# Causal attention in a two-block kernel: scores laid out with keys on the partitions instead of queries

## The chip, the cores and the metric

The program runs on 1 core of one Trainium2 chip. The metric is the device time of one execution in microseconds (us); lower is better.

## The reference, cut to what matters

The kernel computes two blocks in float32: first a mixer of two linear recurrences over 2048 tokens, then a block with latent attention, a spatial gating unit and an output projection. Only the attention of the second block is touched. It has 8 heads; a query or key of a head has 64 + 32 = 96 entries, a value 64:

```python
def one_block(args):
    qi, i = args
    sc = jnp.einsum('bqhd,bkhd->bhqk', qi, k).astype(jnp.float32) * scale
    qpos = i * Q_BLOCK + jnp.arange(Q_BLOCK)
    mask = kpos[None, :] <= qpos[:, None]
    sc = jnp.where(mask[None, None], sc, -jnp.inf)
    p = jax.nn.softmax(sc, axis=-1).astype(v.dtype)
    return jnp.einsum('bhqk,bkhd->bqhd', p, v)
```

## The kernel before, in words

The program is a row of phases, each a block of its own in which the engines run hand-written queues, with semaphores between them. `phase_attention` is the last but one; `phase_output` follows when it has ended. A helper `Stages` gives each step of an engine a number on that engine's semaphore; a `wait_ge(X.sem, X.at(0, name))` waits for the step called `name`. Eight PSUM banks of 512 float32 columns are shared out by hand.

`phase_attention` first makes all values (`vall`, line 3161), then works through four pairs of heads. For a pair it projects queries and keys ("P": 8 ring items of 128x512, lines 3170 and 3174, copied to `qT` and `kT` by ScalarE at line 3244). Its scores ("S", line 3187) have 128 queries on the partitions and up to 512 keys as columns; p counts pairs of query blocks, e the two heads of the pair, r the two query blocks. VectorE takes each piece out of PSUM, scales it and keeps a maximum per query (L3308), adds the causal mask to the diagonal piece (L3313), and reduces the maxima (L3317, L3320). ScalarE takes the exponent of a whole row of pieces at once, with the maximum as its bias and the row's sum as a by-product (L3253). The rest of the work ("R") turns each 128x128 tile of exponents on TensorE (L3204), so that keys come to the partitions, copies it to SBUF on ScalarE (`pT`, L3266), and multiplies it with the values (L3217). The two heads' results go to the two halves of a bank's partitions. At the end of an R the reciprocals of the sums are spread by four small matmuls (L3222), copied (L3274) and multiplied onto the result (L3327).

The order of S and R steps is written out by hand and alternates long and short rows, so that VectorE and ScalarE work on the scores of one step while TensorE turns and multiplies those of another. Three banks hold scores (`NS`), three hold turned tiles (`NTB`), two hold results. GpSimd has nothing to do in this phase but to build the mask.

## Time and profile before

| what | value |
|---|---|
| median of 3 runs | 4113.3 us (4111.99 to 4114.04) |
| the profiled execution, its own time | 4112.49 us |
| its span, first to last instruction | 4110.8 us |
| TensorE busy in the span | 3831.5 us, 93% |
| VectorE, ScalarE, GpSimd busy | 2097.6 us, 1295.6 us, 705.6 us |
| TensorE's mean granted clock | 0.970 |

Times below are microseconds from the span's start. Engines: PE is TensorE's matmul queue, PEld its weight loads, DVE VectorE, ACT ScalarE, POOL GpSimd, SP the queue that issues DMAs. A float32 matmul shows as two records; a transpose as one. Records of matmuls overlap, so a busy time divided by the count, or the distance between starts, is a price, and the mean duration is not.

### The profile page before, as it was taken

To read this page: it belongs to the slowest core of one execution; us is meant where nothing else is said; L and a number is where in the kernel's file an instruction comes from. 1 tells how busy PE (TensorE), PEld (TensorE's weight loads), DVE (VectorE), ACT (ScalarE), POOL (GpSimd) and SP (SyncE) were. 2 spreads that over 40 slices of the span, in tenths; PEclk is the share of its full clock that TensorE was granted. 3 is DMA by queue.
4 is the path that set the end of the run, shared out by engine and by line. 5 is a ranking of instruction groups with operands and counts; after the bars stand their busy time and mean duration, and the time that the engine had idled before them with its cause. 6 is when DMAs were issued, how large, how long until landed. Compare 5 with 4: busy or idle time off the path is not lost. (4 is left out here: it accounts for less than half of the span.)

```text
span 4110.8 us, 48844 instructions
## 1 busy us (share of the span) xinstructions
PE 3831.5 (93%) x18971; PEld 1967.7 (48%) x18971; DVE 2097.6 (51%) x3541; ACT 1295.6 (32%) x2539; POOL 705.6 (17%) x660
## 2 busy tenths in 40 slices
PE   6999899998799989999999899898989799999898
PEld 3444354454577764444444344344544355555443
DVE  7688337543566656122227767524445343443377
ACT  3333132553455547111110001111221355555400
POOL 0000010000566640032114231212200000000031
PEclk8999999999999999999999999899989999999999
DMA  5222582576555544122325633321120000000133
GB/s 192 47 51 48 99 175 81 131 130 114 167 170 172 173 130 139 62 87 82 125 83 175 200 118 108 118 82 41 41 62 12 22 1 8 8 1 6 69 121 108
DMA packets 590152, 386.33 MB, mean 94 GB/s; under 512 B 412019, under 2 KB 525783, under 8 KB 586979
## 3 DMA queue, kind: packets, MB, share of 16 engines
q1 hardware_dynamic: 573059, 315.57, 27.9%
q0 software_dynamic: 10336, 42.47, 2.9%
q10 hardware_dynamic: 6528, 25.17, 1.5%
q8 instruction: 152, 2.49, 0.3%
q14 instruction: 77, 0.63, 0.1%
HBM read 252.59 MB, written 130.55 MB: 93 GB/s over the span
## 5 line engine op out<-in xcount | busy, mean ns | idle before, releaser
L635 PE MATMUL bank<-uT,front_W 128*128 128x512 f32 (+1 forms) x1216 | 488.0, 563 | 4.9 <-ACT front_b_ L842 4.9
L567 PE MATMUL bank<-uT,front_W 128*128 128x512 f32 (+1 forms) x896 | 363.1, 563 | 0.0
L635 PEld LDWEIGHTS bank<-uT,front_W 128*128 128x128 f32 x1216 | 231.9, 192 | 252.5 <-issue 246.1
L567 PEld LDWEIGHTS bank<-uT,front_W 128*128 128x128 f32 x896 | 169.8, 191 | 182.8 <-issue 179.5
L3187 PE MATMUL bank<-kT,attn_qT 96*128 96x512 f32 (+3 forms) x640 | 250.1, 543 | 7.4 <-ACT kT L3244 6.8
L1613 PE MATMUL bank<-uT 128*128 128x512 f32 x512 | 224.3, 596 | 4.3 <-PEq L1186 4.3
L3266 ACT ACTIVATE attn_pT<-bank 128x512 f32<-128x512 f32 (+1 forms) x288 | 157.6, 574 | 124.9 <-PE bank L3204 123.4
L3187 PEld LDWEIGHTS bank<-kT,attn_qT 96*128 96x128 f32 x640 | 114.8, 192 | 131.7 <-issue 76.7
L1312 POOL TENSOR_TENSOR scan_U<-scan_U,gla_w 128x512 f32<-128x512 f32 x144 | 146.7, 1039 | 167.8 <-DVE scan_U L1500 167.8
L3217 PE MATMUL bank<-attn_pT,uT 128*64 128x256 f32 (+1 forms) x1152 | 169.2, 389 | 6.4 <-ACT attn_pT L3266 6.4
L3308 DVE TENSOR_SCALAR_CACHE_REDUCE attn_sc_big<-bank 128x512 f32<-128x512 f32 (+1 forms) x208 | 126.0, 627 | 89.5 <-PE bank L3187 87.5
L3327 DVE TENSOR_TENSOR uT<-bank,attn_spread 128x256 f32<-128x256 f32 x32 | 13.6, 425 | 288.3 <-ACT attn_spread L3274 288.3
L1613 PEld LDWEIGHTS bank<-uT 128*128 128x128 f32 x512 | 96.5, 191 | 119.9 <-issue 119.9
L1302 POOL TENSOR_TENSOR scan_SP<-scan_S,eGl 128x512 f32<-128x512 f32 x144 | 146.6, 1039 | 26.2 <-DVE scan_S L1519 19.7
L1012 DVE RECIPROCAL front_q<-front_q 128x2048 f32<-128x2048 f32 (+1 forms) x8 | 110.0, 13752 | 47.5 <-ACT front_q L789 47.5
L3253 ACT ACTIVATE attn_sc_big<-attn_sc_big,attn_top 128x1920 f32<-128x1920 f32 (+3 forms) x64 | 104.3, 1629 | 94.8 <-DVE attn_top L3320 94.8
L3415 POOL TENSOR_TENSOR out_S<-uT,out_b 128x512 f32<-128x512 f32 x8 | 10.1, 1264 | 709.2 <-DVE uT L3495 709.2
L3204 PE MATMUL bank<-ident,attn_sc_big 128*128 128x128 f32 x800 | 126.2, 286 | 1.2 <-ACT attn_sc_big L3253 1.2
L1519 DVE TENSOR_TENSOR scan_S<-scan_SP,bank 128x512 f32<-128x512 f32 x144 | 92.5, 684 | 63.2 <-PE bank L1394 63.2
L1004 DVE SCALAR_TENSOR_TENSOR front_work<-front_work,front_taps 128x2308 f32<-128x2308 f32 (+1 forms) x48 | 121.6, 2533 | 1.7
L1785 PE MATMUL bank<-yT,merge_S 128*128 128x512 f32 x256 | 117.7, 603 | 4.0 <-POOL merge_S L1772 4.0
L3204 PEld LDWEIGHTS bank<-ident,attn_sc_big 128*128 128x128 f32 x800 | 86.3, 142 | 68.5 <-issue 55.0
(546 smaller groups left out, 6937.3 us busy)
## 6 DMA issues: line engine op xcount, KB each, us to landing
scan_gq<-gla_asks_keys_values SPq DMA_DIRECT2D x36, 768.0 KB, 7.6
scan_dq<-delta_qkv SPq DMA_DIRECT2D x32, 768.0 KB, 6.3
merge_gates<-merge_r ACTq DMA_DIRECT2D x16, 1024.0 KB
uT<-merge_gates SPq DMA_DIRECT2D x16, 1024.0 KB, 9.0
gla_asks_keys_values<-front_a SPq DMA_DIRECT2D x14, 1152.0 KB, 11.2
front_W<-in_w_in SPq DMA_DIRECT2D x28, 512.0 KB, 10.7
delta_qkv<-front_b_ SPq DMA_DIRECT2D x8, 1152.0 KB, 9.9
gla_asks_keys_values<-front_b_ SPq DMA_DIRECT2D x8, 1152.0 KB, 17.7
```

The lines of the kernel that those rows point to most:

```text
L567: m = pe.matmul(bank[:, conv_bank(f, b), 0:n], W[:, f % 2, k, :], uT[:, k, t0:t0 + n], start=(k == 0), stop=(k == KT - 1))
L635: mm = pe.matmul(bank[:, b, 0:n], W[:, s, k, :], uT[:, k, t0:t0 + n], start=(k == 0), stop=(k == KT - 1))
L1004: dve.scalar_tensor_tensor(out=acc[:, lo:WIDE], in0=raw[:, f % 2, lo + t:t + WIDE], scalar=tap[:, t:t + 1], in1=acc[:, lo:WIDE], op0=ALU.m ...
L1302: nc.gpsimd.tensor_tensor(SP[d][:], S[d][:], bcast(gl, 2, P), ALU.mult).then_inc(GS(f"SP{d}"), 1)
L1312: nc.gpsimd.tensor_tensor(U[d][:], U[d][:], bcast(w, 2, P), ALU.mult).then_inc(GU(f"U{d}"), 1)
L1613: mm = pe.matmul(bank[:, b, :], W[f % 2][:, k, :], uT[:, k, CTX + b * BANK:CTX + (b + 1) * BANK], start=(k == 0), stop=(k == KT - 1))
L1785: mm = pe.matmul(bank[:, spot(q, name), :], left[:, k, :], right(k), start=(k == 0), stop=(k == H - 1))
L3187: pe.matmul(bank[:, SC0 + ring[name] % NS, 0:hi - lo], qT[:, e, i * P:(i + 1) * P], kT[0:QK, e, lo:hi], start=True, stop=True).then_inc(TS ...
L3204: m = pe.transpose(bank[:, TB0 + n % NTB, (2 * e + r) * P:(2 * e + r + 1) * P], tile_of(p, e, r)[:, c * P:(c + 1) * P], chip.ident[:])
L3217: m = pe.matmul(bank[e * DV:(e + 1) * DV, ob, r0:2 * P], vall[:, c, h * DV:(h + 1) * DV], pT[:, n % NTB, e, r0:2 * P], start=(c == 0), sto ...
L3266: act.activation(pT[:, n % NTB, :, r0:2 * P], bank[:, TB0 + n % NTB, :].rearrange("p (e t) -> p e t", e=2)[:, :, r0:2 * P], ACT.Copy).then ...
L3308: m = dve.tensor_scalar(t[:, g * BANK:g * BANK + w], bk[:, 0:w], SCALE, None, ALU.mult, ALU.max, accum_out=mx[:, s, u, plain:plain + 1])
```

## The change

The scores of `phase_attention` are made the other way round: 128 keys (a chunk c) on the partitions, and up to 512 queries (a quarter B of the sequence) as columns. The work is cut into 32 units (`UNITS`), each one head and one quarter, in the order B = 3, 0, 3, 0, 2, 1, 2, 1 in each pair of heads; a unit has 4(B + 1) chunks, the last four of them cut to 512, 384, 256 and 128 columns by the causal edge. For each chunk:

- TensorE makes the scores in one of four ring banks (`NS = 4`);
- VectorE adds the mask in PSUM to the first 128 columns of an edge chunk, then takes an elementwise maximum of the chunk with a running one in `mx`;
- ScalarE copies the scores to SBUF; only this frees the ring bank.

At the end of a unit's scores TensorE turns the four 128-wide parts of `mx` (`turn`), VectorE reduces them to one exact maximum per query (`top`), and TensorE spreads these to a full bank (`tops`). Then, again per chunk, VectorE subtracts that bank from the scores, ScalarE takes the exponent with the scale, GpSimd adds the exponents into `acc` (512 wide, one add after the other), and TensorE multiplies them with the values, queries as columns, in two halves of 256. After the last chunk `total` sums `acc` over the partitions with a matmul against ones, and VectorE's `out` takes a 256-wide reciprocal and multiplies it onto both halves.

The values of unit u are interleaved with the scores of unit u + 1 (`merged` for TensorE; `led` for VectorE and ScalarE, four chunks ahead). `total` of unit u stands in the middle of unit u + 1, `out` of unit u at its end. The tile that holds the scores and exponents is one of two, `sc[u % 2]`; the ScalarE copy of unit u's first chunk therefore waits for the last value matmul and the last GpSimd add of unit u - 2.

```diff
-    NS, NTB = 3, 3
-    SC0, TB0, OB0 = 0, 3, 6
-    BIG, SMALL = QT // 2 - 1, QT // 4 - 1
+    PER_B = BANK // P
+    HB = BANK // 2
+    NS, TB, MB, OB = 4, 4, 5, 6
+    AHEAD = 4
+    UNITS = [(h, B) for a in range(PAIRS) for h, B in ((2 * a, 3), (2 * a, 0), (2 * a + 1, 3), (2 * a + 1, 0),
+                                                      (2 * a, 2), (2 * a, 1), (2 * a + 1, 2), (2 * a + 1, 1))]
+    NU = len(UNITS)
+    chunks = lambda B: range(PER_B * (B + 1))
+
+    def cut(B, c):
+
+        d = max(0, c - PER_B * B)
+        start = min(c, PER_B * B) * BANK + sum(BANK - n * P for n in range(d))
+        return d * P, start, BANK - d * P
+    size = lambda B: sum(cut(B, c)[2] for c in chunks(B))
+
+    def items(u):
+
+        if u == NU:
+            return []
+        h, B = UNITS[u]
+        first = [("proj", k, h // 2, b) for b in range(NB) for k in "qk"] if u % (NU // PAIRS) == 0 else []
+        return first + [("score", u, c) for c in chunks(B)]
+
+    def merged(u):
+
+        X, Y = items(u + 1)[3:], [("value", u, c) for c in chunks(UNITS[u][1])]
+        R, X = X[:3], X[3:]
+        while X or Y:
+            if X and (not Y or len(X) * len(chunks(UNITS[u][1])) >= len(Y) * max(1, len(items(u + 1)) - 6)):
+                R.append(X.pop(0))
+            else:
+                R.append(Y.pop(0))
+        R.insert(len(R) // 2, ("sum", u - 1))
+        return R
+
+    def led(u):
+
+        Y = [("value", u, c) for c in chunks(UNITS[u][1])]
+        lead = Y[:AHEAD]
+        R = merged(u)
+        out, early = [], 0
+        for x in R:
+            if x[0] == "value":
+                if x[2] + AHEAD < len(Y):
+                    out.append(Y[x[2] + AHEAD])
+            elif x[0] != "sum":
+                if early < len(lead):
+                    out.append(lead[early])
+                    early += 1
+                out.append(x)
+            if x[0] == "value" and early < len(lead):
+                at = len(out) - (1 if x[2] + AHEAD < len(Y) else 0)
+                out[at:at] = lead[early:]
+                early = len(lead)
+        return out
+
+    ring_items = [x for u in range(-1, NU) for x in items(u + 1)]
+    ring = {x: i for i, x in enumerate(ring_items)}
+    name = lambda x: "_".join(str(v) for v in x)
...
-        sc = [sb("sc_big", [P, 2, (4 * BIG + 3) * P]), sb("sc_small", [P, 2, (4 * SMALL + 3) * P])]
-        pT = sb("pT", [P, NTB, 2, 2 * P])
-        mx = sb("mx", [P, 2, 4, 5])
-        top, total, share = (sb(n, [P, 2, 4]) for n in ("top", "total", "share"))
-        spread = sb("spread", [P, 2 * P])
+        sc = [sb("sc_big", [P, size(3)]), sb("sc_small", [P, size(1)])]
+        mx = sb("mx", [P, 2, BANK])
+        acc = sb("acc", [P, 2, BANK])
+        top = sb("top", [P, 2, PER_B])
+        share = sb("share", [P, HB])
...
-        order = []
-        for a in range(PAIRS):
-            order += [("P", a, 0), ("S", a, 7)] + ([("R", a - 1, 3)] if a else [])
-            order += [(x, a, p) for x, p in (("S", 0), ("R", 7), ("S", 6), ("R", 0), ("S", 1), ("R", 6), ("S", 5), ("R", 1),
-                                            ("S", 2), ("R", 5), ("S", 4), ("R", 2), ("S", 3), ("R", 4))]
-        order.append(("R", PAIRS - 1, 3))
...
+        def piece(x):
+            _, u, c = x
+            lo, start, w = cut(UNITS[u][1], c)
+            return lo, sc[u % 2][:, start:start + w], w
+        spot = lambda x: ring[x] % NS
 
...
-                                    pattern=[[-1, P]], channel_multiplier=1).then_inc(mask_ready, 1)
+                                    pattern=[[1, P]], channel_multiplier=-1).then_inc(mask_ready, 1)
+            for u in range(NU):
+                for c in chunks(UNITS[u][1]):
+                    x = ("value", u, c)
+                    lo, p, w = piece(x)
+                    if c == 0 and u >= 2:
+                        pool.wait_ge(TH.sem, TH.at(0, str(u - 2)))
+                    if c:
+                        pool.wait_ge(GP.sem, GP.at(0, name(("value", u, c - 1))))
+                    pool.wait_ge(AX.sem, AX.at(0, name(x)))
+                    if c:
+                        pool.tensor_tensor(acc[:, u % 2, lo:BANK], acc[:, u % 2, lo:BANK], p, ALU.add).then_inc(GP(name(x)), 1)
+                    else:
+                        pool.tensor_copy(acc[:, u % 2, :], p).then_inc(GP(name(x)), 1)
 
...
-            def rest(a, p):
...
-                                m = pe.transpose(bank[:, TB0 + n % NTB, (2 * e + r) * P:(2 * e + r + 1) * P],
-                                                 tile_of(p, e, r)[:, c * P:(c + 1) * P], chip.ident[:])
...
+            def item(x):
+                n = ring[x] - NS
+                if n >= 0:
+                    pe.wait_ge(AE.sem, AE.at(0, name(ring_items[n])))
...
+                    m = pe.matmul(dst[:, 0:w], kT[0:QK, h % 2, c * P:(c + 1) * P], qT[:, h % 2, B * BANK + lo:(B + 1) * BANK],
                                   start=True, stop=True)
...
+            def turn(u):
+                pe.wait_ge(DM.sem, DM.at(0, name(("score", *last_of(u)[1:]))))
+                if u:
+                    pe.wait_ge(DT.sem, DT.at(0, str(u - 1)))
+                else:
+                    pe.wait_ge(vall_copied, QT)
+                for t in range(PER_B):
+                    m = pe.transpose(bank[:, TB, t * P:(t + 1) * P], mx[:, u % 2, t * P:(t + 1) * P], chip.ident[:])
+                m.then_inc(TT(str(u)), 1)
+
+            def tops(u):
+                pe.wait_ge(DT.sem, DT.at(0, str(u)))
+                if u:
+                    pe.wait_ge(DS.sem, DS.at(0, name(last_of(u - 1))))
+                for t in range(PER_B):
+                    m = pe.matmul(bank[:, MB, t * P:(t + 1) * P], top[:, u % 2, t:t + 1].broadcast_to([P, P]), chip.ident[:],
+                                  start=True, stop=True)
+                m.then_inc(TM(str(u)), 1)
+
+            def value(x):
+                _, u, c = x
+                h, B = UNITS[u]
+                lo, p, w = piece(x)
+                pe.wait_ge(AX.sem, AX.at(0, name(x)))
+                if c == 0 and u >= 2:
+                    pe.wait_ge(DO.sem, DO.at(0, str(u - 2)))
+                for half in range(2):
+                    q0 = max(lo, half * HB)
+                    if q0 < (half + 1) * HB:
+                        m = pe.matmul(bank[half * DV:(half + 1) * DV, OB + u % 2, q0 - half * HB:HB],
+                                      vall[:, c, h * DV:(h + 1) * DV], p[:, q0 - lo:(half + 1) * HB - lo], start=(c == 0),
+                                      stop=(c == PER_B * B + 2 * half + 1))
+                m.then_inc(TO(name(x)), 1)
+
+            def total(u):
+                if u < 0:
+                    return
+                pe.wait_ge(GP.sem, GP.at(0, name(last_of(u))))
+                for half in range(2):
+                    m = pe.matmul(bank[half * DV:(half + 1) * DV, OB + u % 2, HB:BANK], chip.ones[:, 0:DV],
+                                  acc[:, u % 2, half * HB:(half + 1) * HB], start=True, stop=True)
+                m.then_inc(TH(str(u)), 1)
+
+            for x in items(0):
+                item(x)
+            for u in range(NU):
+                X = items(u + 1)
+                for x in X[:1]:
+                    item(x)
+                turn(u)
+                for x in X[1:3]:
+                    item(x)
+                tops(u)
+                for x in merged(u):
+                    if x[0] == "value":
+                        value(x)
+                    elif x[0] == "sum":
+                        total(x[1])
+                    else:
+                        item(x)
+            total(NU - 1)
 
...
-            def exponents(a, p, tiles):
...
-                    act.activation(t, t, ACT.Exp, bias=top[:, slot(p), u], accum_out=total[:, slot(p), u]
...
-            def rest(a, p, scored):
...
+                    _, u, c = x
+                    lo, p, w = piece(x)
+                    if c == 0 and u >= 2:
+                        act.wait_ge(TO.sem, TO.at(0, name(last_of(u - 2))))
+                        act.wait_ge(GP.sem, GP.at(0, name(last_of(u - 2))))
+                    act.wait_ge(DM.sem, DM.at(0, name(x)))
+                    m = act.activation(p, bank[:, spot(x), 0:w], ACT.Copy)
+                m.then_inc(AE(name(x)), 1)
+
+            for x in items(0):
+                item(x)
+            for u in range(NU):
+                for x in items(u + 1)[:3]:
+                    item(x)
+                for x in led(u):
+                    if x[0] == "value":
+                        lo, p, w = piece(x)
+                        act.wait_ge(DS.sem, DS.at(0, name(x)))
+                        act.activation(p, p, ACT.Exp, scale=SCALE).then_inc(AX(name(x)), 1)
+                    else:
+                        item(x)
 
...
-            def rest(a, p):
...
+            def item(x):
+                if x[0] == "proj":
+                    return
+                _, u, c = x
+                h, B = UNITS[u]
+                lo, p, w = piece(x)
+                d = c - PER_B * B
+                bk = bank[:, spot(x), 0:w]
+                dve.wait_ge(TS.sem, TS.at(0, name(x)))
+                if d >= 0:
+                    dve.tensor_tensor(bk[:, 0:P], bk[:, 0:P], ahead[:], ALU.add).then_inc(DK(f"{u}_{d}"), 1)
+                    dve.wait_ge(DK.sem, DK.at(0, f"{u}_{d}"))
+                if c:
+                    dve.wait_ge(DM.sem, DM.at(0, name(("score", u, c - 1))))
+                    dve.tensor_tensor(mx[:, u % 2, lo:BANK], bk, mx[:, u % 2, lo:BANK], ALU.max).then_inc(DM(name(x)), 1)
+                else:
+                    dve.tensor_copy(mx[:, u % 2, :], bk).then_inc(DM(name(x)), 1)
+
+            def out(u):
+                if u < 0:
+                    return
+                h, B = UNITS[u]
+                dve.wait_ge(TH.sem, TH.at(0, str(u)))
+                if u:
+                    dve.wait_ge(DO.sem, DO.at(0, str(u - 1)))
+                dve.reciprocal(share[:], bank[:, OB + u % 2, HB:BANK]).then_inc(DH(str(u)), 1)
+                dve.wait_ge(DH.sem, DH.at(0, str(u)))
+                e = h % 2
+                for half in range(2):
+                    rows = slice(half * DV, (half + 1) * DV)
+                    m = dve.tensor_tensor(oT[e * DV:(e + 1) * DV, h // 2, B * BANK + half * HB:B * BANK + (half + 1) * HB],
+                                          bank[rows, OB + u % 2, 0:HB], share[rows, :], ALU.mult)
+                m.then_inc(DO(str(u)), 1)
+
+            for x in items(0):
+                item(x)
+            for u in range(NU):
+                X = items(u + 1)
+                for x in X[:1]:
+                    item(x)
+                dve.wait_ge(TT.sem, TT.at(0, str(u)))
+                dve.tensor_reduce(top[:, u % 2, :], bank[:, TB, :].rearrange("p (t k) -> p t k", k=P), mybir.AxisListType.X, ALU.max
+                                  ).then_inc(DT(str(u)), 1)
+                for x in X[1:3]:
+                    item(x)
+                dve.wait_ge(TM.sem, TM.at(0, str(u)))
+                for x in led(u):
+                    if x[0] == "value":
+                        lo, p, w = piece(x)
+                        dve.wait_ge(AE.sem, AE.at(0, name(("score", *x[1:]))))
+                        dve.tensor_tensor(p, p, bank[:, MB, lo:BANK], ALU.subtract).then_inc(DS(name(x)), 1)
+                    else:
+                        item(x)
+                out(u - 1)
+            out(NU - 1)
```

## Rows read from the trace of the kernel before

**Rows 1.** Window over the phase: PE, PEld, DVE, ACT, POOL busy, granted clock.
```profile
3259.80:3884.80 625.00, 609.13 (x3233) 328.30 (x3231) 258.59 (x1024) 359.50 (x642) 0.00 (x0) 0.99 0.02 4
```

**Rows 2.** TensorE's groups in the phase: count, busy us, mean ns.
```profile
L3204 PE MATMUL bank<-ident,attn_sc_big 128*128 128x128 f32 x800 | 126.2, 286 | 1.2 <-ACT attn_sc_big L3253 1.2
...
L3222 PE MATMUL bank<-ident,attn_share 128*64 128x128 f32 x256 | 21.0, 279 | 0.0
...
L3187 PE MATMUL bank<-kT,attn_qT 96*128 96x128 f32 x64 | 12.8, 282 | 0.2 <-DVE attn_sc_big L3313 0.2
```

**Rows 3.** Timeline of TensorE: start, us, engine, line, instructions merged.
```profile
3259.82 1.88 PE L3170 MATMUL bank<-cqT,attn_WQ 128*128 128x512 f32 x4
3261.53 1.02 PE L3174 MATMUL bank<-ckvT,attn_WK 128*128 128x512 f32 x2
...
3420.70 15.24 PE L3187 MATMUL bank<-kT,attn_qT 96*128 96x512 f32 x32 [1.70 <-ACT kT L3244]
...
3878.28 0.66 PE L3204 MATMUL bank<-ident,attn_sc_small 128*128 128x128 f32 x4
3878.87 0.65 PE L3217 MATMUL bank<-attn_pT,uT 128*64 128x256 f32 x4
3879.45 0.66 PE L3204 MATMUL bank<-ident,attn_sc_small 128*128 128x128 f32 x4
```

**Rows 4.** VectorE's groups, by form, whole span.
```profile
L3313 DVE SCALAR_TENSOR_TENSOR attn_sc_big<-bank,attn_ahead 128x128 f32<-128x128 f32 x64 | 18.3, 287 | 0.0
...
L3327 DVE TENSOR_TENSOR uT<-bank,attn_spread 128x256 f32<-128x256 f32 x32 | 13.6, 425 | 288.3 <-ACT attn_spread L3274 288.3
...
L3031 DVE RECIPROCAL latents_v<-latents_v 128x1024 f32<-128x1024 f32 x4 | 26.2, 6553 | 0.1
...
L3325 DVE RECIPROCAL attn_share<-attn_total 128x4 f32<-128x4 f32 x32 | 5.4, 168 | 0.0
```

**Rows 5.** Timeline in the scans, GpSimd and VectorE side by side.
```profile
1319.24 2.04 POOL L1312 TENSOR_TENSOR scan_U<-scan_U,gla_w 128x512 f32<-128x512 f32 x2 [2.46 <-DVE scan_U L1500]
...
1320.54 1.28 DVE L1519 TENSOR_TENSOR scan_S<-scan_SP,bank 128x512 f32<-128x512 f32 x2 [0.85 <-PE bank L1394]
```

**Rows 6.** ScalarE's groups of the phase, by form.
```profile
L3266 ACT ACTIVATE attn_pT<-bank 128x512 f32<-128x512 f32 x256 | 146.5, 598 | 118.2 <-PE bank L3204 116.7
...
L3253 ACT ACTIVATE attn_sc_small<-attn_sc_small,attn_top 128x512 f32<-128x512 f32 x8 | 5.8, 720 | 0.0
...
L3253 ACT ACTIVATE attn_sc_small<-attn_sc_small,attn_top 128x128 f32<-128x128 f32 x8 | 3.2, 396 | 0.0
```

**Rows 7.** GpSimd: timeline of the output phase; L3417 needs L3415's result.
```profile
3912.48 1.27 POOL L3415 TENSOR_TENSOR out_S<-uT,out_b 128x512 f32<-128x512 f32 x1 [3.37 <-DVE uT L3495]
3913.83 1.27 POOL L3417 TENSOR_TENSOR out_S<-out_S,uT 128x512 f32<-128x512 f32 x1
```

**Rows 8.** GpSimd at half the width, by form.
```profile
L482 POOL TENSOR_TENSOR front_work<-front_neg_beta,ctri 128x256 f32<-128x256 f32 x18 | 12.5, 718 | 593.1 <-DVE front_neg_beta L1068 511.1 <-DMA delta_blocks<-front_work 82.0
```

**Rows 9.** Windows of 2 us; granted clock third from last.
```profile
3422.00:3424.00 2.00, 2.00 (x4) 0.85 (x3) 1.32 (x4) 0.00 (x0) 0.00 (x0) 0.60 0.00 0
3424.00:3426.00 2.00, 2.00 (x4) 0.97 (x3) 0.88 (x3) 0.00 (x0) 0.00 (x0) 0.55 0.00 0
...
3578.00:3580.00 2.00, 2.00 (x6) 0.95 (x5) 1.74 (x5) 0.00 (x0) 0.00 (x0) 1.00 0.02 4
```

**Rows 10.** Windows of 4 us after the phase's end.
```profile
3888.00:3892.00 4.00, 0.00 (x0) 0.00 (x0) 1.23 (x1) 0.00 (x0) 0.54 (x1) 0.50 1.05 362
...
3896.00:3900.00 4.00, 4.00 (x6) 1.68 (x5) 0.20 (x1) 0.00 (x0) 0.50 (x1) 0.50 1.04 387
```

**Rows 11.** Timeline, output phase: VectorE adds from SBUF alone, without and with GpSimd.
```profile
3902.46 2.29 DVE L3560 TENSOR_TENSOR out_WT<-uT,out_WT 128x2048 f32<-128x2048 f32 x1 [0.38 <-DMA uT<-in_w_out]
...
3902.57 6.55 POOL L3426 TENSOR_TENSOR uT<-uT 128x2048 f32<-128x2048 f32 x1 [6.07 <-DMA uT<-in_w_out]
...
3904.86 6.40 DVE L3563 TENSOR_TENSOR out_WT<-uT,out_WT 128x2048 f32<-128x2048 f32 x1
```

230 lines of the change are left out of this document (44 added, 186 removed).

## Prediction, made before the changed kernel ran

> **What bounds the kernel now.** I read the page's engine shares first (TensorE 93% busy), then the windows over the attention phase, then its groups, then timelines for the spacing of starts. Attention lasts from 3259.8 to 3884.8 us: 625 us, of which TensorE is busy for 609, ScalarE for 360, VectorE for 259 and GpSimd for none [rows 1]. TensorE sets the pace; in 625 us it is without work for 16. The other phases are not touched, so the change is worth what it does to these 625 us.
>
> **TensorE's work.** The scores have as many columns as before (136 x 128 per head, 320 matmuls), and the values too (two streams to two halves of the partitions, as now). A 512-column matmul costs 0.86 us, since the four records of a projection start 1.71 us before the next [rows 3]. A step of four value records costs 0.58 and a step of four turns 0.59 by their starts [rows 3]. What goes: 1088 turns, of which the 800 in the first row cost 126 us busy [rows 2]; by the starts 0.146 each, 159 us. Also the 32 spreads of shares (21 us busy, 19 after overlap) [rows 2]. What comes, for each of 32 units: four turns of the maxima (0.6); four 128x128 spreads of them, eight records between 0.08 (share spreads, 64 columns wide) and 0.2 us (128-column scores) [rows 2], that is 0.7 to 1.6, taken at 1.2 because the full width loads twice the weights of the one; and a sum of the exponents (0.6). That is 2.4 a unit, 77 in all. TensorE: 609 - 159 - 19 + 77 = 508 us.
>
> **VectorE's work.** Each chunk costs a maximum and a subtraction, each with one PSUM input. The trace has this shape: two 512-wide adds with a PSUM input in 1.28 us [rows 5], 0.64 each; 128 columns take 0.29 [rows 4]; between them I interpolate 0.40 and 0.52. Then 224 x 0.64 + 96 x 0.40 = 181 us, twice: 363. The 128 mask additions, each followed by a wait for itself, 0.33: 42. Per unit a reduction over 512 columns (0.69), two 256-wide multiplications (0.43 each) and a 256-wide reciprocal. Today's reciprocals are 4 wide (0.17 us); one of 1024 takes 6.55 [rows 4], so 256 columns cost about 0.17 + 252 x 6.26 ns = 1.75. That is 3.3 a unit, 105 in all. VectorE: 510 us, nearly TensorE's 508, where it now has 259.
>
> **ScalarE and GpSimd.** A copy of 512 columns takes 0.60, an exponent 0.72 and a 128-wide one 0.40 [rows 6]: copies 172, exponents 209, projections 38, together 419 us. GpSimd: an add that needs the one before starts 1.35 us after it [rows 7]; 256 columns take 0.72 [rows 8]. The scans' adds take 1.02 each, with one operand broadcast [rows 5]. The changed adds have two full operands and form a chain through `acc`, so I take 1.35 and keep 1.02 as the lower bound. 192 full adds, 96 narrow ones at 0.8 and 32 copies at an estimated 0.6 are 357 us. No engine is over-full, but the queues are in order, so the units have to be walked.
>
> **One boundary.** Let 0 be VectorE's last maximum of a unit's scores. VectorE is next in `out` of an older unit (1.75 + 0.85 = 2.6), then takes the next unit's first maximum (0.65), so `top` is ready at 4.0. TensorE, which by then has done the turn and two scores, idles 1.5 to 2 us. VectorE's next two maxima and TensorE's `tops` both end at about 5.4, the subtraction at 6.1, the first exponent at 6.8. Where the next unit starts with an edge chunk its masks add 0.5: 7.3.
>
> **Units B = 3 with scores B = 0 (8 of them).** From 5.9 VectorE subtracts a chunk every 0.65 and ScalarE exponentiates one every 0.72: all 16 are out by about 18.5. GpSimd needs 0.6 + 12 x 1.35 + 2.5 = 19.3 from 7.3 on and ends at 26.6. Behind it stands ScalarE: its first copy of the unit after next reuses the tile, so it waits until 26.6. Its queue then holds all exponents, too. TensorE can put four scores in the ring and stops at about 21; VectorE stops as well. From 27 on TensorE has the rest of the B = 3 scores (9.0), the four values (1.7) and a sum (0.65): 11.4, and with VectorE's last maximum the pair of units takes 39.2. Where scores B = 2 follow it is four scores less: 35.8.
>
> **The other units.** v2 with scores 1, and v1 with scores 2: VectorE's sums are 15.9 each, boundary included, with the last hand-overs 16.3, 17.2 and 16.4 (GpSimd's lag, 5 us after the first of them, costs 1 in the second). v1 with projections and scores 3: TensorE 30.7, walked 31. One pair of heads: 39.2 + 35.8 + 16.3 + 17.2 + 16.4 + 31 = 155.9. All: projections and first scores 26, four pairs 623.6, less the last 31, plus a tail of 18, less 3 (no `out` in the first unit): 634 us at full clock. Taken with adds at 1.02, the eight B = 3 units give back 8 x 12 x 0.33 = 32: 602.
>
> **TensorE's clock.** Now it is granted 0.99 over the phase [rows 1], for it hardly idles. After the 1.70 us gap at 3419 the clock showed 0.60 and 0.55 for two windows of 2 us [rows 3, 9]; after an equal gap at 3576 it stayed at 1.00 [rows 9]. At half clock (1.2 instead of 2.4 GHz) such a stretch of some 3 us costs 1.4 us of work. After the long pause behind the phase the clock was at 0.50, and still there in the first 4 us of continuous work [rows 10]. The change makes one gap of 1.5 to 2 us in each of 32 units and one of about 5.5 behind each of the 8 long chains of adds. The long ones end where TensorE has the critical part, at 2.4 each (4 us and somewhat more at half clock): 8 x 2.4 = 19. Of the short ones I take half, and of these only some 4 us in all, since in most units VectorE or GpSimd is the longer: 22 together, bounds 0 and 45. The Trainium skill ("TensorE: Matmul & The Clock Gate", section on HAM oscillation) speaks against the change: it says that waits between short blocks of matmuls re-throttle the engine, so that every block begins cold. The trace bears that out for one of the two equal gaps named here. With that rule at all 32 boundaries the sum would be near the upper bound instead of 22.
>
> **The sum.** 634 + 22 = 656 against 625: +31. The profiled execution took 4112.5, 0.8 under the median of 4113.3; with 1.7 outside its span that does not change. 4112.5 + 31 = 4143.5, rounded to 4144.
>
> **Edits at no cost.** The mask's other triangle is built once, before the phase's first score, behind the value matmuls; were it not covered it would be under 1 us. SP's DMAs are the same; their waits name the same moments (last projection, last score of a pair). The wait for the rotated queries existed before (part of the 1.70 us gap).
>
> **Rivals.**
> - *The accumulation hides, and the time falls* (0.24). One mechanism: GpSimd's chain of adds keeps up with the exponents. For it: GpSimd's total is 357 of more than 550 us, and the scans show 1.02 for an add [rows 5]. Against: dependent adds with two full operands are at 1.35 [rows 7]. It decides where an add costs under about 0.85, or where the tile's next use came later than walked. Then units 1 to 4 take VectorE's 16.3 each: 155.9 - (75 - 65.2) = 146 a pair, 595; with queues that slide ideally VectorE's 510 plus four projections at 10: 550. At little clock loss 595 gives 4082, 550 gives 4038; the middle, 4060.
> - *Everything cancels* (0.08): adds at 1.02 and the clock's 22 give 624: 4111.
> - *The clock falls at every boundary* (0.10): 32 x 1.4 instead of the short gaps' 4, and the long ones 19 to 25: about +65 to +75, 4185.
> - *VectorE and GpSimd get in each other's way* (0.03). A VectorE add with both inputs in SBUF took 2.29 us alone and 6.40 beside a GpSimd add that took 6.55 [rows 11]. If it were so here, VectorE's 363 us and GpSimd's 357 would queue behind one another: some 170 more than VectorE's bound, 4240 or above. Against: with one PSUM input both kept their price side by side [rows 5], and the change has no VectorE operation with two SBUF inputs. The Trainium skill ("GPSIMD Engine Reference", SBUF interfaces) says the same: contention comes with two SBUF inputs or a 2-port mode. By that rule the sum stays as it is.
>
> **Chances and range.** My forecast has 0.55, for 4122 to 4175: below by adds at 1.2 us, above by 45 us of clock losses. Faster 0.24, same 0.08, clock 0.10, contention 0.03. A change within 0.2% (8 us) can't be told from none. Slower: 0.55 + 0.10 + 0.03 = 0.68. Eight in ten: from 4068 (leaves out half of the faster cases) to 4190 (most of the clock case is in).
>
> **What would show it.** Right: ScalarE's copy from PSUM waits on GpSimd in 8 units, those that follow a B = 3, for 4 to 8 us; GpSimd at 1.3 us per add; the reciprocal at 1.75 us; VectorE busy for about 510 us of the phase and TensorE for about 510 plus what the clock adds, granted clock 0.93 to 0.97. Wrong: waits on GpSimd under 2 us (the first rival), VectorE's 512-wide operations above 0.8 us beside GpSimd (the last), or a reciprocal that is a lot cheaper, which would shorten each boundary and VectorE's total by up to 50 us.

## The result, and the profile after

The changed kernel takes 4209.4 us (median of 4 runs, 4203.16 to 4221.19) against 4113.3 (4111.99 to 4114.04): ratio 1.0237, 95% interval 1.0214 to 1.026. It is 96 us slower, 65 more than forecast and beyond the range's upper end of 4190. The profiled execution, read below, is the fastest of the four (4203.16).

The window over the attention phase, with its last reductions (the columns are those of [rows 1]):

```profile
3261.00:3975.00 714.00, 595.35 (x2401) 279.71 (x2399) 491.81 (x896) 366.10 (x706) 333.21 (x320) 0.87 0.02 4
```

The phase lasts 713.9 us, from 3261.0 to 3974.9; it was 625 [rows 1]. TensorE is busy for 595 of them, but at a granted clock of 0.87: part of that is work at half clock (1.2 instead of 2.4 GHz). VectorE went from 259 to 492. No engine is full any more.

The groups of the phase, by form, answering to [rows 2, 4, 6, 7]:

```profile
L3218 PE MATMUL bank<-attn_qT,kT 96*128 96x512 f32 x448 | 261.0, 705 | 57.5 <-ACT attn_sc_big L3307 47.1 <-ACT kT L3298 10.3
L3183 POOL TENSOR_TENSOR attn_acc<-attn_acc,attn_sc_big 128x512 f32<-128x512 f32 x160 | 203.7, 1273 | 22.5 <-ACT attn_sc_big L3319 11.4
L3341 DVE TENSOR_TENSOR attn_mx<-bank,attn_mx 128x512 f32<-128x512 f32 x192 | 132.7, 691 | 124.9 <-PE bank L3218 121.2
L3377 DVE TENSOR_TENSOR attn_sc_big<-attn_sc_big,bank 128x512 f32<-128x512 f32 x176 | 109.7, 679 | 2.8 <-PE bank L3237 2.8
L3319 ACT ACTIVATE attn_sc_big<-attn_sc_big 128x512 f32<-128x512 f32 x176 | 106.4, 630 | 9.4 <-DVE attn_sc_big L3377 8.6
L3307 ACT ACTIVATE attn_sc_big<-bank 128x512 f32<-128x512 f32 x176 | 103.0, 600 | 227.4 <-POOL attn_acc L3183 113.6 <-DVE attn_mx L3341 103.5 <-DVE attn_mx L3343 7.1
L3352 DVE RECIPROCAL attn_share<-bank 128x256 f32<-128x256 f32 x32 | 56.0, 1749 | 3.9 <-PE bank L3261 3.9
```

The last part of a row is the idle time in front of the group. In all, ScalarE's copies (L3307) stood 114 us behind GpSimd's adds (L3183) and 104 behind maxima. The scores (L3218) stood 47 us behind those copies; the same 448 records cost 261 us here and 222 in a variant at clock 0.96 (experiment 4).

The timeline of one unit, the first B = 3, after its scores had ended at 3286 (columns as in [rows 3]):

```profile
3293.04 7.46 ACT L3319 ACTIVATE attn_sc_big<-attn_sc_big 128x512 f32<-128x512 f32 x15
...
3293.81 18.54 POOL L3183 TENSOR_TENSOR attn_acc<-attn_acc,attn_sc_big 128x512 f32<-128x512 f32 x15 [0.17 <-ACT attn_sc_big L3319]
...
3312.44 1.57 ACT L3307 ACTIVATE attn_sc_big<-bank 128x512 f32<-128x512 f32 x3 [11.94 <-POOL attn_acc L3183]
3313.09 5.05 PE L3218 MATMUL bank<-attn_qT,kT 96*128 96x512 f32 x6 [6.28 <-ACT attn_sc_big L3307]
```

This is the walk's central picture. ScalarE has all exponents out at 3300.5, GpSimd adds them until 3312.4, ScalarE's next copy waits 11.9 us for the tile, and TensorE 6.3 us for the copy. Eight chains end like this one, and TensorE's stalls behind them last 4.9 to 6.3 us, 44 in all. TensorE then needs 5.05 us for six records that take 2.84 at full clock: it came back at half speed. Windows around that restart (granted clock third from last), and around the same restart in the third pair of heads:

```profile
3313.00:3315.00 2.00, 1.91 (x3) 0.88 (x4) 0.00 (x0) 2.00 (x6) 0.41 (x1) 0.50 0.00 0
3315.00:3317.00 2.00, 2.00 (x4) 0.97 (x3) 1.11 (x3) 1.32 (x4) 1.23 (x3) 0.50 0.00 0
3317.00:3319.00 2.00, 2.00 (x7) 0.49 (x6) 1.49 (x3) 0.90 (x3) 1.12 (x2) 0.86 0.00 0
...
3659.00:3661.00 2.00, 1.95 (x3) 0.92 (x4) 0.00 (x0) 2.00 (x6) 0.38 (x1) 0.50 0.00 0
3661.00:3663.00 2.00, 2.00 (x4) 0.93 (x3) 1.15 (x3) 1.29 (x3) 1.23 (x2) 0.50 0.00 0
3663.00:3665.00 2.00, 2.00 (x6) 0.30 (x4) 1.18 (x3) 0.79 (x2) 1.18 (x2) 0.50 0.01 4
3665.00:3667.00 2.00, 2.00 (x6) 0.84 (x3) 0.27 (x1) 0.60 (x1) 0.00 (x0) 0.50 0.00 0
3667.00:3669.00 2.00, 2.00 (x3) 0.34 (x1) 0.69 (x1) 0.60 (x1) 0.00 (x0) 0.50 0.00 0
3669.00:3671.00 2.00, 2.00 (x9) 0.94 (x8) 0.69 (x1) 0.60 (x1) 0.00 (x0) 0.50 0.01 4
3671.00:3673.00 2.00, 2.00 (x4) 1.03 (x4) 0.02 (x1) 0.00 (x0) 0.00 (x0) 0.61 0.00 0
3673.00:3675.00 2.00, 2.00 (x6) 0.57 (x4) 1.67 (x3) 1.03 (x2) 0.00 (x0) 1.00 0.00 0
```

The first restart is at full clock again after some 4.5 us. The second, after a gap of nearly the same length (6.08 us), keeps TensorE at 1.2 GHz for 13 us of continuous work. By the starts of `top`'s reductions (L3368) the units from there to the next ones last, in us:

| kernel | u0 | u1 | u2 | u3 | u4 | u5 | u6 | u7 | pair |
|---|---|---|---|---|---|---|---|---|---|
| forecast, full clock | u0+u1 39.2 | | u2+u3 35.8 | | 16.3 | 17.2 | 16.4 | 31 | 155.9 |
| after, pair 1 | 15.1 | 29.1 | 15.3 | 24.4 | 15.4 | 18.5 | 15.7 | 36.2 | 169.6 |
| after, pair 2 | 15.7 | 28.6 | 15.7 | 24.3 | 15.4 | 18.5 | 15.7 | 42.3 | 176.2 |
| after, pair 3 | 15.4 | 33.1 | 16.3 | 27.5 | 15.4 | 18.5 | 15.7 | 42.3 | 184.3 |

The granted clock is 0.7 to 0.9 in u0 to u3, 1.00 in u4 to u6, and in u7 1.00 in the first pair and 0.84 in later ones. Equal queues, unequal times: that is the clock's part. The rest is the same in every pair. The fourth pair repeats the third up to u5 and has no u7.

### The profile page after: what moved, and what is told of

Read it like the earlier page. It is cut to its first block and busy times, and to the rows that moved or that the text cites. A ratio compares the mean times of both kernels' runs of the same rounds, so it can differ in the third digit from the quotient of the medians.

```text
span 4201.5 us, 47760 instructions
## 1 busy us (share of the span) xinstructions
PE 3818.2 (91%) x18139; PEld 1918.9 (46%) x18139; DVE 2330.1 (55%) x3413; ACT 1301.2 (31%) x2603; POOL 1041.2 (25%) x980
## 5 line engine op out<-in xcount | busy, mean ns | idle before, releaser
L3218 PE MATMUL bank<-attn_qT,kT 96*128 96x512 f32 (+3 forms) x640 | 314.5, 615 | 57.5 <-ACT attn_sc_big L3307 47.1
L3183 POOL TENSOR_TENSOR attn_acc<-attn_acc,attn_sc_big 128x512 f32<-128x512 f32 (+3 forms) x208 | 238.4, 1146 | 26.2 <-ACT attn_sc_big L3319 11.4
L3341 DVE TENSOR_TENSOR attn_mx<-bank,attn_mx 128x512 f32<-128x512 f32 (+3 forms) x288 | 173.4, 602 | 128.2 <-PE bank L3218 121.2
L3218 PEld LDWEIGHTS bank<-attn_qT,kT 96*128 96x128 f32 x640 | 119.3, 211 | 181.6 <-issue 82.4
L3307 ACT ACTIVATE attn_sc_big<-bank 128x512 f32<-128x512 f32 x224 | 121.4, 554 | 243.0 <-DVE attn_mx L3341 117.9
L482 POOL TENSOR_TENSOR front_work<-front_neg_beta,ctri 128x256 f32<-128x256 f32 x18 | 12.5, 716 | 593.9 <-DVE front_neg_beta L1068 512.0
L1302 POOL TENSOR_TENSOR scan_SP<-scan_S,eGl 128x512 f32<-128x512 f32 x144 | 146.7, 1039 | 26.2 <-DVE scan_S L1519 19.7
L3251 PE MATMUL bank<-attn_sc_big,uT 128*64 128x256 f32 (+1 forms) x832 | 129.0, 433 | 22.9 <-ACT attn_sc_big L3319 22.8
L3377 DVE TENSOR_TENSOR attn_sc_big<-attn_sc_big,bank 128x512 f32<-128x512 f32 x224 | 126.2, 622 | 2.8 <-PE bank L3237 2.8
L3319 ACT ACTIVATE attn_sc_big<-attn_sc_big 128x512 f32<-128x512 f32 x224 | 121.9, 581 | 9.8 <-DVE attn_sc_big L3377 8.6
L1818 ACT ACTIVATE merge_r<-merge_r 128x1024 f32<-128x1024 f32 x32 | 33.7, 1052 | 268.4 <-DVE merge_r L1865 266.0
```

What stands on the lines that cost most here:

```text
L1302: nc.gpsimd.tensor_tensor(SP[d][:], S[d][:], bcast(gl, 2, P), ALU.mult).then_inc(GS(f"SP{d}"), 1)
L3183: pool.tensor_tensor(acc[:, u % 2, lo:BANK], acc[:, u % 2, lo:BANK], p, ALU.add).then_inc(GP(name(x)), 1)
L3218: m = pe.matmul(dst[:, 0:w], kT[0:QK, h % 2, c * P:(c + 1) * P], qT[:, h % 2, B * BANK + lo:(B + 1) * BANK], start=True, stop=True)
L3251: m = pe.matmul(bank[half * DV:(half + 1) * DV, OB + u % 2, q0 - half * HB:HB], vall[:, c, h * DV:(h + 1) * DV], p[:, q0 - lo:(half + 1) * ...
L3319: act.activation(p, p, ACT.Exp, scale=SCALE).then_inc(AX(name(x)), 1)
L3341: dve.tensor_tensor(mx[:, u % 2, lo:BANK], bk, mx[:, u % 2, lo:BANK], ALU.max).then_inc(DM(name(x)), 1)
```

## The experiments

Ratios are to the kernel before, with 95% intervals; times are medians. Kernels that build on one another show only the new edit.

**1. Idle time filled.** TensorE multiplies into banks that nobody reads at that moment, before `tops`, before the first values, in the stall and before the first score after projections, so that it never rests long:

```diff
+            def fill(n, bk):
+                for _ in range(n):
+                    pe.matmul(bank[:, bk, :], chip.ident[:], cqT[:, 0, 0:BANK], start=True, stop=True)
...
+                if u:
+                    pe.wait_ge(DS.sem, DS.at(0, name(last_of(u - 1))))
+                    fill(2, MB)
                 tops(u)
-                for x in merged(u):
+                for i, x in enumerate(merged(u)):
+                    if i == 1 and u + 1 < NU:
+                        if len(X) == PER_B:
+                            fill(2, TB)
+                        elif UNITS[u - 1][1] == 3:
+                            fill(7, TB)
+                    if x[0] == "score" and x[2] == 0:
+                        fill(3, TB)
```

> The changed kernel with idle-time matmuls added (all results kept): 2 before each spread of the maxima, 2 before the first value of a unit whose successor has quarter 0, 7 where the wait for GpSimd's chain is, 3 before the first score after projections; identity times 512 columns, into banks that are free there. Theory 'half clock is the missing term': the phase took 714 us where 634 were walked at full clock; the granted clock of the phase goes from 0.87 to above 0.97 and the time falls by 45 to 75 us, to 4135 to 4165. Rival 'the missing time is full-clock waiting, and the low clock only goes with it': the clock rises but the time falls by less than 20 us, or rises.

Measured: 4168.9, ratio 1.0139 (1.0124 to 1.0154). Its phase lasts 683 us, from 3258 to 3942; a window that begins 3 us late and ends 8 us behind it:

```profile
3261.00:3950.00 689.00, 649.54 (x2684) 300.35 (x2683) 491.46 (x897) 368.14 (x704) 334.61 (x321) 0.99 0.03 7
```

The clock is back at 0.99 and every pair lasts 169.8 us. Useless work makes the kernel 40 us faster, a little less than the 45 to 75 expected. Yet a pair is still 13.9 over the forecast, so the clock is not all, or the fills cost something themselves. Experiments 3 and 4 part the two.

**2. GpSimd's adds made cheap.** One column instead of up to 512, on a tile preset to ones; the sum of the exponents is left out.

```diff
-                        pool.tensor_tensor(acc[:, u % 2, lo:BANK], acc[:, u % 2, lo:BANK], p, ALU.add).then_inc(GP(name(x)), 1)
+                        pool.tensor_tensor(acc[:, u % 2, lo:lo + 1], acc[:, u % 2, lo:lo + 1], p[:, 0:1], ALU.add).then_inc(GP(name(x)), 1)
...
-                        pool.tensor_copy(acc[:, u % 2, :], p).then_inc(GP(name(x)), 1)
+                        nc.gpsimd.memset(acc[:, u % 2, :], 1.0).then_inc(GP(name(x)), 1)
```

> The changed kernel with GpSimd's adds 1 column wide instead of 512 to 128, on a tile preset to 1.0: this leaves out the sum of the exponents. All waits stay. Theory 'GpSimd's chain holds ScalarE': the 12 waits of ScalarE for GpSimd (113.6 us) go, the units behind quarter 3 fall from 28.6 to 33.1 and 24.3 to 27.5 us to some 17 to 20, and the time falls by 70 to 110 us, to 4100 to 4140. Rival 'VectorE and the hand-overs bound those units anyway': the time falls by less than 35 us.

Measured: 4112.7, ratio 1.0004 (0.9994 to 1.0013). The chain of adds, with what it does to the clock, is worth 97 us, as much as the whole slowdown. u1 and u3 fall to 20.3 and 16.0; u0 and u2 stay at 15.4 and 15.6. Not all is well without the chain: u7, with projections, lasts 41.1 to 42.5 at a clock of 0.84 to 0.88, where the first pair of the changed kernel had 36.2 at 1.00.

**3. Both.** Cheap adds, and the fills but for the seven in the stall, which no longer exists.

> The narrow adds and the added matmuls together, without the group of 7 (leaves out the sum of the exponents). If the clock is also lost without GpSimd's chain, in the short gaps at the boundaries, this is 15 to 40 us faster than narrow adds alone; if only the long waits bring the clock down, it is within 8 us of it or slower.

Measured: 4118.0, ratio 1.0016 (1.0007 to 1.0025), 5 us slower than without fills, at clock 1.00 in every unit. This is a balance, and no sign that the gaps cost nothing. By the starts of `top`'s reductions, the full clock makes u0 and u2 14.6 us long instead of 15.1 to 15.6 (7 us in eight units) and u7 37.9 instead of 41.1 to 42.5 (11 us in three). Against that u1, u3 and u5 each last 1.7 us longer (20 us in twelve), the time of the two fills in front of `tops`, and u6 0.5. So the short gaps behind which the clock falls cost some 0.8 us each, and the gap before the first score after projections costs more.

**4. Fills in the long gaps alone.** Six in the stall, two before the first score after projections, nothing at the boundaries.

```diff
+                        if len(X) > PER_B and UNITS[u - 1][1] == 3:
+                            fill(6, TB)
+                    if x[0] == "score" and x[2] == 0:
+                        fill(2, TB)
```

> The changed kernel with idle-time matmuls only in its long gaps (6 at the wait for GpSimd's chain, 2 before the first score after projections), none at the short gaps before the spread of the maxima and before the first value. All results kept. If the long gaps bring the clock down, this is at or below the 4169 of all fillings, with a granted clock of the phase above 0.95; if the short gaps do it as well, the clock of the phase stays near 0.9 and the time between 4175 and 4205.

Measured: 4151.7, ratio 1.0098 (1.0083 to 1.0113), 58 us faster than the changed kernel. Its phase, of 665.0 us (from 3258.3 to 3923.3), and two of its groups, the fills themselves being the second:

```profile
3258.20:3924.00 665.80, 592.19 (x2513) 284.27 (x2511) 490.27 (x896) 363.87 (x707) 333.90 (x320) 0.96 0.02 4
```
```profile
L3218 PE MATMUL bank<-attn_qT,kT 96*128 96x512 f32 x448 | 222.4, 612 | 9.7 <-ACT attn_sc_big L3322 6.1 <-ACT kT L3313 3.5
...
L3243 PE MATMUL bank<-cqT,ident 128*128 128x512 f32 x112 | 50.0, 592 | 0.0
```

This is the changed kernel's course without the clock losses behind its long gaps: 713.9 - 665.0 = 49 us of the profiled phase was clock (58 by the medians). The fills hardly delay the scores behind them, since TensorE still waits for ScalarE's copies there, 6.1 us in all. The third pair is 15.5, 25.8, 15.3, 21.7, 15.4, 18.5, 15.8 and 36.2: 164.2. Taken unit by unit, 36 of the 49 us lie in u1 and u3, behind the stalls, and 12 in the u7 of the second and third pair. The short gaps are not filled here: u0 and u2 last 15.1 to 16.5 us at a clock mostly of 0.78, against 14.6 in experiment 1, some 7 us more in eight units.

**5. What the turns had cost.** In the kernel before, one turn per chunk instead of up to four, its copy 16 columns wide, and the values multiplied with a preset tile. Most of the turning and copying is left out.

```diff
-                        for e, r in TILES:
+                        for e, r in TILES[:1] if c < length(p, 0) else TILES[1:2]:
...
-                    act.activation(pT[:, n % NTB, :, r0:2 * P],
-                                   bank[:, TB0 + n % NTB, :].rearrange("p (e t) -> p e t", e=2)[:, :, r0:2 * P], ACT.Copy
+                    act.activation(pT[:, n % NTB, 0, r0:r0 + 16], bank[:, TB0 + n % NTB, r0:r0 + 16], ACT.Copy
```

> The kernel before, with one turn of a tile per chunk instead of two to four and ScalarE's copy 16 columns wide; the values are multiplied with a preset tile: leaves out most of the turning. Theory 'the removed turns were on the path': 272 of 1088 to 288 turns stay, some 110 us of TensorE work go, and the time falls by 85 to 115 us, to 4000 to 4030. Rival 'VectorE or ScalarE take over at once': less than 50 us.

Measured: 4039.5, ratio 0.9825 (0.981 to 0.9839): -72, less than the -85 to -115 expected. The groups tell why:

```profile
L3207 PE MATMUL bank<-ident,attn_sc_big 128*128 128x128 f32 x208 | 61.3, 320 | 1.2 <-ACT attn_sc_big L3257 1.2
...
L3270 ACT ACTIVATE attn_pT<-bank 128x16 f32<-128x16 f32 x288 | 47.5, 181 | 144.7 <-PE bank L3207 143.8
```

208 turns standing alone are busy for 61 us, 0.29 each, where the 800 of [rows 2] have 0.16; and TensorE stands 13 us behind the copies:

```profile
L3220 PE MATMUL bank<-attn_pT,uT 128*64 128x256 f32 x1024 | 168.9, 418 | 14.3 <-ACT attn_pT L3270 12.8
```

Turning and copying were on the path all the same: the change removes something real.

**6. `out` taken earlier.** VectorE's reciprocal and multiplications at three quarters of a unit instead of at its end, to shorten the boundary.

```diff
-                for x in led(u):
+                L = led(u)
+                for i, x in enumerate(L):
+                    if i == 3 * len(L) // 4:
+                        out(u - 1)
...
-                out(u - 1)
```

> The changed kernel, all results kept, with VectorE's `out` (reciprocal 1.75 us, two multiplications 0.86) moved from the end of a unit, ahead of the next boundary, to three quarters of the unit. Theory 'it stands in the chain of the boundary': units that end in a chain (behind quarter 3, and the one with projections) lose 2.6 us each at their boundary, and TensorE's gap before the spread of the maxima shrinks, so that the clock falls less: 20 to 50 us faster than the changed kernel. Rival 'VectorE's sum bounds the units, wherever the 2.6 us stand': within 10 us of it.

Measured: 4200.8, ratio 1.0215 (1.0188 to 1.0242), 9 us under the changed kernel, whose own runs span 18: a miss. VectorE's wait for a unit's first scores, in the changed kernel and then in this one (us in total, times, longest; the longest is the one before the phase's first scores):

```profile
DVE attn_mx L3343 <- PE bank L3218: 68.9, 10, 36.2
```
```profile
DVE attn_mx L3343 <- PE bank L3218: 106.9, 20, 36.1
```

The boundary did get shorter: the first exponent of a B = 3 ends 4.3 to 5.7 us after the last maximum instead of 6.9 to 7.7 (the phase's first unit apart), and ScalarE's waits for GpSimd fell from 114 us to 72. But part of `out` had filled a time in which VectorE would wait for TensorE, and in the middle of a unit it lies before subtractions that are wanted. TensorE's waits for exponents, in the changed kernel and then in this one:

```profile
PE bank L3251 <- ACT attn_sc_big L3319: 22.8, 32, 2.4
```
```profile
ACT attn_sc_big L3307 <- POOL attn_acc L3183: 71.6, 8, 11.9
...
PE bank L3251 <- ACT attn_sc_big L3319: 64.7, 54, 2.6
```

By units, u3 lasts 16.7 to 21.2 us (24.3 to 27.5 before) and u5 16.2 (18.5), while u0, u2, u4 and u6, some 15.5 before, last mostly 18.8 to 20.7. Gain and loss are nearly equal.

**7. Another order of the units.** B = 3, 3, 2, 2, 1, 1, 0, 0 instead of 3, 0, 3, 0, 2, 1, 2, 1, with two tiles of full size. Between a B = 3 and the next use of its tile there is now the work of a unit of like size instead of a B = 0, so GpSimd has longer until the tile is wanted.

```diff
-    UNITS = [(h, B) for a in range(PAIRS) for h, B in ((2 * a, 3), (2 * a, 0), (2 * a + 1, 3), (2 * a + 1, 0),
-                                                      (2 * a, 2), (2 * a, 1), (2 * a + 1, 2), (2 * a + 1, 1))]
+    UNITS = [(h, B) for a in range(PAIRS) for h, B in ((2 * a, 3), (2 * a + 1, 3), (2 * a, 2), (2 * a + 1, 2),
+                                                      (2 * a, 1), (2 * a + 1, 1), (2 * a, 0), (2 * a + 1, 0))]
...
-        sc = [sb("sc_big", [P, size(3)]), sb("sc_small", [P, size(1)])]
+        sc = [sb("sc_big", [P, size(3)]), sb("sc_small", [P, size(3)])]
```

> The changed kernel, all results kept, with the quarters of a pair of heads in the order 3, 3, 2, 2, 1, 1, 0, 0 instead of 3, 0, 3, 0, 2, 1, 2, 1, and two tiles of the large size for the scores. The values of quarter 3 then lie beside 16 or 12 scores, and the unit is longer than GpSimd's chain of 19.3 us. Theory 'the chain is exposed by the order': ScalarE's waits for GpSimd fall from 114 us to under 20, a pair of heads from 176 to some 150, and the kernel is 90 to 140 us faster than the changed one, 4070 to 4120. Rival 'each in-order boundary costs the same wherever it stands, and short units beside short ones have more of it for their work': a gain under 40 us.

Measured: 4083.6, ratio 0.9941 (0.9924 to 0.9958): 126 us faster than the changed kernel, and 0.6% faster than the one before. Its phase, of 594.0 us, then its waits:

```profile
3259.00:3851.00 592.00, 533.11 (x2399) 252.69 (x2397) 487.25 (x894) 367.33 (x705) 334.19 (x320) 0.99 0.02 4
```
```profile
ACT attn_sc_small L3307 <- POOL attn_acc L3183: 61.3, 11, 6.0
...
PE bank L3218 <- ACT kT L3298: 6.9, 4, 1.7
PE bank L3218 <- ACT attn_sc_small L3307: 5.5, 8, 1.0
PE bank L3218 <- ACT attn_sc_big L3307: 1.8, 4, 0.5
```

The same instructions, but TensorE stays at 0.99 and a pair takes 147. ScalarE still waits on GpSimd, 11 times and at most 6 us (61 us, where under 20 were expected), but TensorE's waits for ScalarE's copies fell from 47.1 to 7.3 us.

**8. That order, and `out` earlier.** Experiments 6 and 7 together.

> Both of these together, all results kept. If the two costs are separate, the gains add, to 4040 to 4100; if the reciprocal was covered by the wait for GpSimd's chain, it gives more here than alone; if VectorE's sum is the bound now, it gives nothing beyond the order.

Measured: 4169.7, ratio 1.0142 (1.0127 to 1.0157): 86 us slower than experiment 7 alone, with the clock down to 0.74 in the small units and a pair at 169; none of the three expectations had this. Here the loss of experiment 6 stands without its gain: moved off the boundary, `out` delays subtractions, and TensorE stands up to 3.2 us before values whose exponents are late.

**9. That order, with cheap adds.** The edits of experiments 7 and 2; the sum of the exponents is left out.

> The reordered kernel (quarters 3, 3, 2, 2, 1, 1, 0, 0) with GpSimd's adds 1 column wide on a tile preset to 1.0; leaves out the sum of the exponents. The reordered kernel still shows 61 us of ScalarE's waits for GpSimd, in 11 places. If they are on the path, the time falls by 15 to 40 us from 4084; if the order has hidden the chain and the waits lie where TensorE has its four scores in the ring, by less than 12.

Measured: 4081.4, ratio 0.9929 (0.9915 to 0.9942), 2 us from experiment 7. What was worth 97 us in the old order is worth nothing measurable in this one: it was never GpSimd's total, but where the chain's end fell. The orders differ without the chain as well: 4112.7 (experiment 2) against 4081.4. So 31 of the 126 us of experiment 7 are not the chain's; some of them are the clock's (u7 lasts 41 to 42 us in experiment 2 and 32.5 in experiment 7), and they are not parted further.

**10. That order, with a reciprocal of one column.** The division by the sums is left out.

```diff
-                dve.reciprocal(share[:], bank[:, OB + u % 2, HB:BANK]).then_inc(DH(str(u)), 1)
+                dve.reciprocal(share[:, 0:1], bank[:, OB + u % 2, HB:HB + 1]).then_inc(DH(str(u)), 1)
```

> The reordered kernel with the reciprocal 1 column wide (about 0.16 us instead of 1.75), the rest of its tile preset to 1.0; leaves out nearly all the division by the sums. Theory 'VectorE works at each boundary while TensorE's last values are still on their way, so that its reciprocal fills a wait': less than 20 of the 51 us that VectorE is spared show in the time. Rival 'VectorE's sum bounds the units': 35 us or more, to 4050 or under.

Measured: 4068.1, ratio 0.9895 (0.9879 to 0.991): -15.5 of the 51 us of VectorE's time that it spares. The rest stood beside waits, as experiments 6 and 8 say of `out` as a whole.

**11. That order, and projections ahead of the exponents in ScalarE's queue**, with two value steps before the first score, against the excess of u7.

```diff
-        R, X = X[:3], X[3:]
+        n = 5 if X and X[0][0] == "proj" else 3
+        R, X = X[:n], X[n:]
+        if n == 5:
+            R, Y = R + Y[:2], Y[2:]
...
-                if early < len(lead):
+                if early < len(lead) and x[0] != "proj":
```

> The reordered kernel, all results kept, with the projections of the next pair ahead of the exponents in ScalarE's queue, and two value steps on TensorE between the last projection and the first score. Theory 'ScalarE's copies of the projections, with four exponents between them, are what the first score waits for': the unit with projections falls from 32.5 to 29 to 31, three times, 4 to 10 us in all. Rival 'TensorE bounds it anyway': under 3 us.

Measured: 4084.5, ratio 0.9937 (0.9924 to 0.9949): no gain. TensorE's timeline behind the last projections shows the new wait, where experiment 7 had 1.73 for `kT`:

```profile
3559.97 1.02 PE L3213 MATMUL bank<-ckvT,attn_WK 128*128 128x512 f32 x2
3563.16 1.08 PE L3254 MATMUL bank<-attn_sc_small,uT 128*64 128x256 f32 x8 [2.17 <-ACT attn_sc_small L3322]
```

The wait moved from `kT` to an exponent and did not go: u7 lasts 32.4 us (34.1 in the first pair), against 32.5. The theory that ScalarE's copies of the projections lengthen u7 found no support.

## Why the prediction was right in kind and too small

Point by point, by the steps of the prediction:

- **The prices** held. Maxima 0.69 and subtractions 0.68 us (0.64 taken), the reciprocal 1.749 (1.75), copies 0.60, adds 1.273 busy and 19.3 to 19.7 us for copy and fifteen adds (19.3 walked). Exponents cost 0.63, not 0.72, and 0.5 on average in a row of fifteen, three of them narrower; they were not on the path. VectorE is busy for 492 (510 forecast), ScalarE 366 (419), GpSimd 333 busy without its hand-overs (357 with them; the terms written there add up to 355).
- **One boundary** held: the first exponent of a B = 3 ends 6.9 us after the last maximum in the first two pairs and 7.7 in the others, 7.3 walked with an edge chunk. But the gap on TensorE, put at 1.5 to 2 us in each of 32 units, was 2.5 in u0 and u2, 1.5 in u4, 1.0 in u6 and nothing to speak of in the others.
- **The chain of adds** held, and is the cause of the slowdown: it ended 26.7 us after the boundary (26.6), 27.5 in the last two pairs, and TensorE stood 4.9 to 6.3 us, 5.5 on average (about 5.5). ScalarE's waits on GpSimd were longer than I wrote (up to 11.9, for 4 to 8) and came after 12 units, not 8: 11.3, 11.3 and 5.7 us per pair, the third behind the first B = 2. Experiments 2, 7 and 9 bear the mechanism out.
- **The failed step is "TensorE's clock".** It had 22 us, bounds 0 and 45; the long gaps alone measured 49 in the profiled phase, 58 by the medians. The eight long gaps behind the chains were priced at 2.4 each, 19 in all, from the 3 to 4 us at half clock seen in [rows 9, 10], and cost 36. In the first two pairs the price was right, 2.5 each by u1 and u3 against experiment 4; in the last two, where the clock stayed at 0.50 for some 13 us instead of 4.5 to 6.3, it was 6.5. The gap before the first score after projections (2.87 us, ending at 3605) had no term: u7 with a clock loss behind it takes 42.3 instead of 36.2, twice, 12 us. The short gaps, given some 4 us, cost some 7 on top of the 49 (u0 and u2, experiments 1 and 4), the step's smallest error. "TensorE: Matmul & The Clock Gate" of the Trainium skill (HAM oscillation) tells of waits of 3 to 5 us for transfers after which each block of matmuls runs slow. The trace agrees for the long gaps: behind all eight, of 4.9 to 6.3 us, the granted clock is 0.50. The prediction laid that rule on gaps of 1.5 to 2 us too, which the page's waits do not cover; that its sum by the rule, near 45, came nearer is in part luck, since most of the loss lay behind the long gaps.
- **The units**, the second term that was sized too small, were 31 us short: 665 (experiment 4) for 634, of which some 7 are the short gaps' clock just named. u7 was walked at 31 and lasts 36.2 (some 16 us in all); u0 + u1 39.2 for 41.3 to 42.2 (10); u2 + u3 35.8 for 37.0 to 37.8 (6). In u1 the walk started TensorE at the end of the chain, but a score first needs a copy out of the full ring, and the timeline of experiment 4 has 14.5 us from the chain's end to the last maximum, where 12.6 were walked. In u7 the walk took TensorE to be busy throughout, for 31. This window holds the first u7 of the changed kernel (columns as in [rows 1]):

```profile
3421.89:3458.07 36.18, 31.33 (x102) 12.87 (x100) 19.36 (x34) 21.62 (x40) 10.12 (x12) 1.00 0.03 6
```

TensorE's 31 us were right, and it is idle for 4.9 more, 2.87 of them before the first score. Whether that idle time can go stays open: experiment 11 only moved it. u4 to u6 were right in sum: 49.7 for 49.9.
- **TensorE's work.** What comes was too small: TensorE is busy for 533 us of experiment 7 at clock 0.99, for 508. Of what goes, experiment 5 shows at least 72 us, of turns and their copies, to have been on the path; the 159 themselves were not measured.
- **Rivals.** "The accumulation hides" is false in this order. Its price was too low as well: experiment 2 is that case, and its phase took 626 us, not 595, for u1 lasts 20.3 (16.3 walked) and u7 41 to 42 (31). In the order of experiment 7 the accumulation does hide, at 594 us, but that 595 was walked for the other order is luck. "The clock falls at every boundary" gave the nearer time, 4185, for the wrong reason: boundaries were cheap and stalls dear (its own terms also give +73 to +79, not +65 to +75). "Everything cancels" needed adds at 1.02; they took 1.27. Contention between VectorE and GpSimd does not show: 0.69 and 1.27 us side by side (and its 4240 does not follow from its terms: 550 + 170 would be 4208).
- **Sum:** 656 forecast; +31 in the units, +27 in the clock behind the long gaps: 714. With the short gaps counted as clock it is some +24 and +34. Both errors point the same way, and the range's upper end took only the clock's bound in, none for a walk that assumes tight hand-overs.

## What to carry to other kernels

When an engine off the path frees a buffer, look at when its chain ends against the buffer's next use, not at its total: here the order of the units alone moved 126 us with the same instructions, and the chain, worth 97 us in one order, was worth 2 in the other. Price a stall on TensorE as its length plus the slow stretch behind it, and take the longest such stretch seen, not the usual one; a stall of 5 to 6 us cost 2.5 us more in two pairs and 6.5 in the others. Before filling a gap, look whether the fill stands on the path: two matmuls in front of `tops` cost their own 1.7 us in u1, u3 and u5. Before moving work away from a boundary, ask which wait it fills, and what is wanted behind its new place.

## What the runs showed of the hardware

TensorE's half-clock stretches after gaps of equal length were unequal: after 6.3 and 6.1 us, 1.2 GHz for some 4.5 and for 13 us of continuous work; after 2.9 us, none that shows in the first pair and about 13 us in the second:

```profile
3605.12 2.05 PE L3218 MATMUL bank<-attn_qT,kT 96*128 96x512 f32 x2 [2.87 <-ACT kT L3298]
...
3608.14 3.78 PE L3218 MATMUL bank<-attn_qT,kT 96*128 96x512 f32 x4
...
3612.91 3.78 PE L3218 MATMUL bank<-attn_qT,kT 96*128 96x512 f32 x4
...
3618.26 1.98 PE L3218 MATMUL bank<-attn_qT,kT 96*128 96x512 f32 x4
```

Four records, two scores, take 3.78 us there and 1.98 once the clock is back. What decides between a short and a long stretch, these runs don't show. At the boundaries the clock fell in u0 and u2, with gaps of 2.5 and 1.0 to 1.3 us close together (unit means mostly 0.78), and stayed at 1.00 in u4 to u6, with gaps of up to 1.5 and 0.7 us. Also unexpected: 56 matmuls that do nothing (112 records, 50 us of TensorE's time) made the kernel 58 us faster.
